# Wide matmuls for every expert tile beside the choice and for ten query tiles a block, with the choice's steps dealt to tiles by their work

## The reference, cut to what matters

```python
q  = einsum('bsd,dk->bsk', h, w_query).reshape(B, S, 8, 2, 128)     # 2048 query columns
sc = einsum('bshpc,hpnc->bshpn', q, sub_keys)                       # 128 scores per head and half
s1, i1 = top_k(sc[..., 0, :], 16);  s2, i2 = top_k(sc[..., 1, :], 16)
top_s, sel = top_k(s1[..., :, None] + s2[..., None, :], 16)         # the choice: 16 experts a head
gates = softmax(top_s)
a   = gelu(einsum('cd,chkd->chk', xc, expert_u[ec])) * gates        # chosen ones of 16384 experts
out = einsum('chk,chkd->cd', a, expert_v[ec])
```

## Time and profile before

| | |
|---|---|
| median of three runs | 2192.66 us |
| the profiled execution's own time | 2192.78 us |
| its span, first to last instruction | 2190.9 us |
| PE, DVE, ACT, POOL busy | 98%, 72%, 58%, 5% of the span |
| mean clock granted to TensorE | 0.991 of full speed |

### The profile page before, as it was taken

One profiled execution on the slowest core, in us unless ns is written; L12 is line 12 of the kernel. 1 busy time (PEld: TensorE's weight loads), 2 busy tenths in 40 slices (PEclk: granted clock), 3 DMA queues, 4 the chain that ended last, 5 costly groups with the idle time before them and its releaser, 6 DMA issues.

```text
span 2190.9 us, 37734 instructions
## 1 busy us (share of the span) xinstructions
PE 2143.4 (98%) x14372; PEld 1941.7 (89%) x14372; DVE 1572.7 (72%) x3423; ACT 1268.0 (58%) x2364; POOL 103.9 (5%) x136
## 2 busy tenths in 40 slices
PE   7999999999999999999999998999999999999998
PEld 5988899898999988888889998999999998888886
DVE  3455658888888867888866655688888887555556
ACT  3355545546999754445545544454579996545554
POOL 0000000404000000000000000004040000000000
PEclk9999999999999999999989999999999999999999
DMA  8665556656443467778744634566554445555664
GB/s 335 204 205 184 176 188 182 191 184 187 127 132 126 156 201 281 283 275 291 255 145 135 204 95 135 184 185 192 183 174 133 127 126 173 182 193 193 193 193 133
DMA packets 110498, 407.49 MB, mean 186 GB/s; under 512 B 11504, under 2 KB 11888, under 8 KB 110064
## 3 DMA queue, kind: packets, MB, share of 16 engines
q1 hardware_dynamic: 98880, 361.81, 51.2%
q10 hardware_dynamic: 11440, 43.28, 5.2%
HBM read 403.99 MB, written 1.05 MB: 185 GB/s over the span
## 4 chain that ended last, share of the span: by engine, by line
PE 91%; DVE 3%; ACT 2%; POOL 2%; issue 1%; DMA 1%; ACTq 0%; DVEq 0%
PE PB L464 24%; PE PB L466 23%; PE PB L465 23%; PE PB L830 6%; PE PB L860 5%; PE PB L858 3%; POOL AR L2303 2%; PE PB L531 1%; PE PB L857 1%; PE PB L802 1%; PE PB L545 1%; PE PB L510 1%; ACT WH L1153 0%; DMA X<-in_x 0%; DVE WL L1604 0%
## 5 line engine op out<-in xcount | busy, mean ns | idle before, releaser
L1604 DVE TENSOR_TENSOR WL<-RING,WH 128x1024 fp32r<-128x1024 f32 x651 | 803.0, 1234 | 477.3 <-ACT WH L1153 475.5
L1153 ACT ACTIVATE WH<-RING 128x1024 fp32r<-128x1024 f32 x651 | 686.6, 1055 | 457.2 <-PE PB L466 454.8
L464 PE MATMUL PB<-HX,WH 128*128 128x256 f32 x2112 | 615.0, 291 | 6.8 <-DVE HX L1659 6.0
L466 PE MATMUL PB<-HX,WL 128*128 128x256 f32 x2112 | 599.5, 284 | 0.0
L465 PE MATMUL PB<-HX,WH 128*128 128x256 f32 x2112 | 599.2, 284 | 0.0
L464 PE MATMUL PB<-WH,HX 128*128 128x512 f32 (+2 forms) x1344 | 494.3, 368 | 7.2 <-DVE HX L1659 3.2
L466 PE MATMUL PB<-WH,HX 128*128 128x512 f32 (+2 forms) x1344 | 490.6, 365 | 0.0
L465 PE MATMUL PB<-WL,HX 128*128 128x512 f32 (+2 forms) x1344 | 490.2, 365 | 0.0
L464 PEld LDWEIGHTS PB<-HX,WH 128*128 128x128 f32 x2112 | 407.0, 193 | 13.1 <-issue 10.1
L465 PEld LDWEIGHTS PB<-HX,WH 128*128 128x128 f32 x2112 | 406.7, 193 | 0.4
L466 PEld LDWEIGHTS PB<-HX,WL 128*128 128x128 f32 x2112 | 405.9, 192 | 0.0
(11 more groups left out here) (233 smaller groups left out, 1849.4 us busy)
## 6 DMA issues: line engine op xcount, KB each, us to landing
RING<-in_u SPq DMA_DIRECT2D x256, 512.0 KB, 3.5
RING<-in_v SPq DMA_DIRECT2D x256, 512.0 KB, 4.2
RING<-in_win SPq DMA_DIRECT2D x90, 512.0 KB, 3.6
AR<-in_wm ACTq DMA_DIRECT2D x40, 1024.0 KB, 6.6
RING<-in_wq SPq DMA_DIRECT2D x32, 512.0 KB, 3.5
AR<-in_wm SPq DMA_DIRECT2D x8, 1024.0 KB, 16.1
RING<-in_wout SPq DMA_DIRECT2D x16, 512.0 KB, 3.5
RING<-in_sk SPq DMA_DIRECT2D x8, 512.0 KB, 3.9
```

The source lines that it names most:

```text
L464: e.matmul(o, ah, bh, start=start, stop=False)
L466: return e.matmul(o, al, bh, start=False, stop=stop)
L1153: e.activation(hi(t), raw(("w", t), words(t)), ACT.Copy).then_inc(s_hi, 1)
L1604: e.tensor_tensor(lo(t), raw(("w", t), words(t)), hi(t).bitcast(F32), ALU.subtract).then_inc(s_lo, 1)
```

## The change

1. All tiles of `u` from 0 to 77 are wide (`WIDE`); tile 78 stays narrow, because the transposes of the choice's results stand in its middle. That is 78 in place of 46 in each block.
2. Of the 16 query tiles of a block the last ten become wide too (`whole`), one tile a bank. ACT copies the second half of the bank, DVE adds the first half.
3. The choice has two more `yield`s: a top-sixteen step falls into two steps, and the work that followed a round's last sum ends in a step of its own. Each step has a number in `CHOICE`, its work, and `choice_turns` deals the steps so that after tile j the share of the work done is (j+1)/77.
4. `scores(1)` stands before tile 36 in place of 39, and the fetches of its two key tiles are three tiles earlier in the plan.

```diff
+CHOICE = [80, 55] * 16 + [110, 150] + [105] * 8 + [55, 120] + [125, 125, 60, 125, 150, 125, 90] + [125, 125, 60, 125, 150, 125]
+CHOSEN = {len(CHOICE) * a + 43: a for a in range(2)}
+def choice_turns():
+    work, turns, n, total = CHOICE * 2, [], 0, 0
+    for j in range(NK):
+        share, count = sum(work) * min(j + 1, JG - 2) / (JG - 2), 0
+        while n < len(work) and total + work[n] <= share + 1e-6:
+            total += work[n]
+            n += 1
+            count += 1
+        turns.append(count)
+    return turns
 def choose_steps(j):
-    return 0 if j >= JG else 2 if j % 32 == 31 else 1
-CHOSEN = {28: 0, 68: 1}
-def wide(j):
-    done = sum(choose_steps(i) for i in range(j + 1))
-    turn = range(done + 1, done + choose_steps(j + 1) + 1)
-    return j < JG - 1 and all((n - 1) % 40 >= 16 for n in turn)
-WIDE = [wide(j) for j in range(NK)]
+    return TURNS[j]
+WIDE = [j < JG - 1 for j in range(NK)]
...
-            if j == 39:
+            if j == 35:
                 plan.extend([("s", 4 * blk + 2), ("s", 4 * blk + 3)])
...
+            def whole(b, n):                                        # PE
+                wh, wl = (t.rearrange("p (k n) -> p k n", k=KT) for t in (hi(n), lo(n)))
+                tile_ready(e, n)
+                for k in range(KT):
+                    if k:
+                        e.matmul(PB[b][:, 0:256], wl[:, k, :], HH[:, k, :], start=False, stop=False)
+                    r = e.matmul(PB[b][:, :], wh[:, k, :], HX[:, k, :], start=k == 0, stop=k == KT - 1)
+                    if k == 0:
+                        e.matmul(PB[b][:, 0:256], wl[:, k, :], HH[:, k, :], start=False, stop=False)
+                r.then_inc(s_used, 1)
...
-                    half(1 + c % 3, 0, n_q + 2 * c, h0 if c == 0 else None)
-                    half(1 + c % 3, 1, n_q + 2 * c + 1)
+                    for t in (2 * c, 2 * c + 1):                    # for c >= 3
+                        ...
+                        whole(1 + t % 3, n_q + t)
...
-                    if j == 39:
+                    if j == 36:
                         scores(1)
...
+                    if c >= 3:                                      # ACT
+                        for t in (2 * c, 2 * c + 1):
+                            fill(n_q + t)
+                            e.wait_ge(s_used, n_q + t + 1)
+                            copy(qP[:, t, :], PB[1 + t % 3][:, 256:512], s_qc)
...
                         if hp % 4 == 3:
                             r.then_inc(s_top, 1)
+                        yield                                       # DVE, choose
                         own.done(t2)
                         r = e.max(vb, SC2[:, i, :])
...
                         own.done(own.mark(e.tensor_tensor(ABF[:, a, 1, :], ABF[:, a, 0, :], GI[:, 2, a, :], ALU.subtract)))
+                        yield
...
+                    if c >= 3:                                      # DVE
+                        for t in (2 * c, 2 * c + 1):
+                            fill(n_q + t)
+                            e.wait_ge(s_qc, 10 * blk + t - 5)
+                            e.tensor_tensor(qP[:, t, :], PB[1 + t % 3][:, 0:256], qP[:, t, :], ALU.add).then_inc(s_qv, 1)
```

## The result

| | before | changed |
|---|---|---|
| median of six runs each | 2191.38 us | 2184.57 us |
| lowest to highest | 2190.72 to 2193.33 | 2182.21 to 2185.57 |
| profiled execution: time, span | 2192.78, 2190.9 | 2185.3, 2183.5 |

The changed kernel takes 0.9965 of the time before, with a 95% interval of 0.9955 to 0.9975: 6.8 us less, or 7.4 by the two spans. The forecast was 4.4 us less than 2192.66, the median of the first three runs; with three more the median before is 2191.38. The new time lies within the range, near its lower end, on the side of rival B.

The account below looks back on a forecast made before the run. PE's pitch was taken to set the time, with DVE next. 2192.8 - 7.0 - 1.8 + 0.5 + 4.0 = 2188.5, rounded to 2188.3 us; range 2184.0 to 2194.0.

Parts of the forecast that it names:

- rival B: Rounds with POOL, comparisons and sums: POOL is in time, so no new stalls on PE; 2184.5 us, chance 0.18.
- the sum waits for POOL until 2.6 + 6.9 = 9.5: Second half's first round, from tile 66's start: comparison done at 2.6, POOL ready 6.9 us later; PE stalls 0.9 at tile 70.
- 84 wide tiles by 0.083, 7.0 us: PE, both blocks: 32 more wide expert tiles and 10 wide query tiles a block save 0.083 us each, 7.0 us.
- The old stalls, 1.8 us: PE's waits for DVE's low part (0.56 us) and at scores(1) (0.34 us) go: 0.90 us a block, 1.8 us.
- The queries' end, +0.5: Before scores(0): ACT's copy plus DVE's add take 0.84 instead of 0.60 us, losing 0.24 a block, 0.5 us.
- The top-sixteen turns: DVE beside the top-sixteen steps: 2.93 us a turn, delay below the 1.9 us of room, no stall, 0.4 us to spare.
- Rival C: Top-sixteen steps: DVE is late if a turn costs 3.05 instead of 2.93 us; 5.4 in all, 2193.9 us, chance 0.17.
- D: Top-sixteen steps: DVE becomes the bound from a turn of 3.11 us on; at 3.2 us, 2202.9 us; chance 0.09.
- The new stalls: Rounds with POOL, second half of tokens: tiles 70 and 76 late by 0.9 and 1.1 us, 2.0 a block, 4.0 us.
- The base: Starting point of the sum: the profiled execution's 2192.8 us, taken as good as the median of 2192.66.
- The rule weighed: Skill's columns / 2.4 plus 2.5 ns for PE matmuls: a wide tile saves 0.02 us, 84 save 1.8, sum 2193.7.

## Why the prediction was wrong in its size

**The step that failed** is "the sum waits for POOL until 2.6 + 6.9 = 9.5", and with it the term of 4.0 us, which measures 1.3 (0.64 a block). I had taken 6.9 us from the earlier trace rows as a time of POOL's own. It was one with four two-input instructions of DVE in it, and the change takes one of them out of just that stretch: the very edit that makes DVE arrive early makes POOL 1.0 us quicker. With 5.9 the same sum has the fill done at 11.0 and no stall at all, which is B. That it came 0.31 late has a second cause, which pulls the other way: the comparison was done 3.0 us after tile 66's start (502.91 to 505.93) and not 2.6, because the add ahead of it waited 0.63 us for ACT. The fill is then done at 12.0 + 0.4 - 1.0 = 11.4, and 11.4 + 0.1 against 11.2 is the measured 0.3 us. In the second round the same two corrections apply: a wait of 2.1 us and a tile 1.1 us late were forecast, 0.98 and 0.21 measured. The clue lay in the trace of before, where POOL's eight multiplies took 11.47 us in this round and 10.48 in another, and the prediction took only the first. These are two POOL rows of the kernel before, in order of time:

```profile
397.55 10.48 POOL L2303 TENSOR_TENSOR AR<-AR 128x256 f32<-128x256 f32 x8 [34.84 <-DVE AR L1933]
413.14 11.46 POOL L2303 TENSOR_TENSOR AR<-AR 128x256 f32<-128x256 f32 x8 [5.11 <-DVE AR L1933]
```

**Point by point.**

- *84 wide tiles by 0.083, 7.0 us: right.* The pitch is 2.797 for the expert tiles wherever none is late. Thirty-two alone gave 2.66 by the rows; with the old deal 2.13 to 2.25 of it arrived, and the key wait that grew took the rest.
- *The old stalls, 1.8 us: right, a little small.* PE waits for neither any more. The late tile cost 0.56 and the one behind it 0.10 more, so 1.0 us a block, 2.0 in all. Here the change's fourth point, which looks like housekeeping, counts: wide tiles without it lose some 0.5 us a block at the key wait.
- *The queries' end, +0.5: right.* From PE's last query matmul to `scores(0)` the gap was 1.01 us and is 1.33, 0.32 a block.
- *The top-sixteen turns: right.* Predicted were 2.93 us a turn, no stall and 0.4 us to spare at turn 54. Measured are 2.92 (adds at 462.52, 465.44, 468.37), no stall, and the fill of tile 56 ends 0.65 us before PE starts it. Rival C is out. The mechanism of D is real, and nearer than I gave it credit for: 0.26 us more a turn costs 13.4 us and makes the kernel slower than before.
- *The new stalls: place right, size three times too large,* as above.
- *The base: 1.3 us too high.* The sum starts from the profiled 2192.8, "as good as the median of 2192.66"; six runs have their median at 2191.38. So 1.3 of the 3.7 us between 2188.3 and 2184.57 are the spread of single runs and no mechanism.
- *The rule weighed: not a fair test.* The section that the prediction names gives columns / 2.4 plus 2.5 ns for an isolated matmul and says that a stream of weight loads and matmuls, as here, keeps another spacing. So the 120 and 350 ns of the earlier trace rows don't speak against the formula, and the sum didn't use it.

With the measured sizes: -7.0 - 2.0 + 0.6 + 1.3 = -7.1, against 7.54 by the stretches and 7.4 by the spans. The 0.4 us between stay without a name; they are no more than the second block's queries vary. Profile against profile, 2192.8 - 7.1 gives 2185.7, and 2185.3 was measured. Rival B gave 2184.5, with no stall at all. That the median came out there is luck: B's sum too starts from the high base, and the trace has the forecast's stalls, a third as long.

## What to carry to other kernels

When a wait of one engine for another is moved, don't take the waited-for time over as a constant: ask which instructions of the waiting engine lie in it and lengthen it, and compare two places of the same trace with different numbers of them. Where two engines go at nearly the same pace, carry the delay turn by turn from a measured cost of a turn; that told here to a quarter of a microsecond what DVE's 90% busy time could not. Work put into a wait is free only if it doesn't slow the engine that is waited for. Start a sum from the middle of several runs when the effect is as small as their spread.

## What the runs showed of the hardware

Each DVE instruction of 1024 columns with two SBUF inputs (1.2 us long by itself) holds up POOL's multiplies by 1.0 us (table above), and one with a single input by nothing that shows (10.48 against 10.47 us for the eight). It goes the other way too: a fill took 1.22 us at 505.93, 1.75 at 508.76 in the midst of POOL's work. The Trainium skill, "SBUF — State Buffer", section "Who interferes with whom", says that a DVE instruction with two SBUF inputs contends with a GpSimd instruction that reads SBUF, and that a `tensor_reduce` on this chip never does; the traces agree with both, and the price per instruction is what they add.
